# Two norms' last squares summed on TensorE, the samples' exponentials one step later, S5's memsets in two steps

## What is computed

```python
def layer_norm(x, g, b):
    xf = x.astype(jnp.float32)
    mu = jnp.mean(xf, -1, keepdims=True)
    var = jnp.mean(jnp.square(xf - mu), -1, keepdims=True)
    y = (xf - mu) * lax.rsqrt(var + LN_EPS) * g.astype(jnp.float32) + b.astype(jnp.float32)
...
    for layer in range(DEPTH):
        xp = layer_norm(DEEPNORM_ALPHA * xp + 0.5 * swiglu(xp, *f1), ln_g[layer, 0], ln_b[layer, 0])
        ...
            attn = moba_sample(qa, ka, va, cache_k[li], cache_v[li], page_table, pos_s)
        ...
        xp = layer_norm(DEEPNORM_ALPHA * xp + mix_p, ln_g[layer, 1], ln_b[layer, 1])
        xp = layer_norm(DEEPNORM_ALPHA * xp + 0.5 * swiglu(xp, *f2), ln_g[layer, 2], ln_b[layer, 2])
```

## Time and profile before

| | us |
|---|---|
| median of 3 runs | 2454.2 |
| lowest, highest | 2453.1, 2458.01 |
| the profiled execution | 2458.37 |
| its span, first to last instruction | 2456.7 |
| mean granted TensorE clock in it | 0.988 of full speed |

### The profile page before, as it was taken

One profiled execution on the slowest core, in us unless ns is written; L12 is line 12 of the kernel. 1 busy time (PEld: TensorE's weight loads), 2 busy tenths in 40 slices (PEclk: granted clock), 3 DMA queues, 4 the chain that ended last, 5 costly groups with the idle time before them and its releaser, 6 DMA issues.

```text
span 2456.7 us, 46764 instructions
## 1 busy us (share of the span) xinstructions
PE 2376.1 (97%) x19043; PEld 2262.7 (92%) x19043; DVE 1633.0 (66%) x2539; ACT 1079.0 (44%) x1632; POOL 463.7 (19%) x531
## 2 busy tenths in 40 slices
PE   9999999999999999999999999999999999999998
PEld 8988998999789878789999999999999998999998
DVE  6898876666665656777677476477556595487555
ACT  3433445433454343442454434454333537354332
POOL 4997700002100012100203001031002010221001
PEclk9999999999999999999999999999999999999999
DMA  8668666445356798544565555555555566555453
GB/s 218 168 185 223 186 195 190 121 117 157 106 149 198 239 311 249 130 131 123 168 173 169 166 180 173 171 167 147 147 154 155 172 196 205 151 168 150 145 152 99
DMA packets 676327, 417.87 MB, mean 170 GB/s; under 512 B 31378, under 2 KB 639602, under 8 KB 676114
## 3 DMA queue, kind: packets, MB, share of 16 engines
q1 hardware_dynamic: 669810, 394.56, 55.7%
q0 software_dynamic: 6304, 20.32, 2.6%
HBM read 396.04 MB, written 18.78 MB: 169 GB/s over the span
## 4 chain that ended last, share of the span: by engine, by line
PE 79%; DVE 13%; ACT 3%; issue 3%; POOL 1%; SPq 0%; DMA 0%; DVEq 0%; ACTq 0%; POOLq 0%
PE ps L271 22%; PE ps L272 21%; PE ps L273 21%; DVE w_lo L266 4%; PE ps L1033 2%; PE ps L1034 2%; PE ps L1035 2%; ACT w_hi L257 2%; PE ps L2442 1%; DVE h_lo L476 1%; PE ps L1770 1%; PE ps L1194 1%; PE ps L2425 1%; PE ps L2388 1%; DVE x L566 1%
## 5 line engine op out<-in xcount | busy, mean ns | idle before, releaser
L266 DVE TENSOR_TENSOR w_lo<-w_raw,w_hi 128x1024 fp32r<-128x1024 f32 (+1 forms) x648 | 831.4, 1287 | 584.4 <-ACT w_hi L257 581.2
L271 PE MATMUL ps<-x_hi,w_hi 128*128 128x256 f32 (+1 forms) x3200 | 967.7, 302 | 23.0 <-DVE w_lo L266 17.4
L272 PE MATMUL ps<-x_lo,w_hi 128*128 128x256 f32 (+1 forms) x3200 | 953.0, 298 | 0.0
L273 PE MATMUL ps<-x_hi,w_lo 128*128 128x256 f32 (+1 forms) x3200 | 952.6, 298 | 0.0
L257 ACT ACTIVATE w_hi<-w_raw 128x1024 fp32r<-128x1024 f32 (+1 forms) x648 | 669.9, 1035 | 548.3 <-PE ps L273 478.1
L271 PEld LDWEIGHTS ps<-x_hi,w_hi 128*128 128x128 f32 x3200 | 612.8, 191 | 41.5 <-DVE w_lo L266 28.0
L272 PEld LDWEIGHTS ps<-x_lo,w_hi 128*128 128x128 f32 x3200 | 613.4, 192 | 1.1 <-issue 0.2
L273 PEld LDWEIGHTS ps<-x_hi,w_lo 128*128 128x128 f32 x3200 | 613.2, 192 | 0.0
L271 PE MATMUL ps<-h_hi,w_hi 128*128 128x256 f32 (+1 forms) x1408 | 423.5, 301 | 11.5 <-DVE w_lo L266 8.0
L273 PE MATMUL ps<-h_hi,w_lo 128*128 128x256 f32 (+1 forms) x1408 | 415.1, 295 | 0.0
L272 PE MATMUL ps<-h_lo,w_hi 128*128 128x256 f32 (+1 forms) x1408 | 415.0, 295 | 0.0
(11 more groups left out here) (287 smaller groups left out, 2172.1 us busy)
## 6 DMA issues: line engine op xcount, KB each, us to landing
w_raw<-in_ffn_w_gate SPq DMA_DIRECT2D x176, 512.0 KB, 3.8
w_raw<-in_ffn_w_up SPq DMA_DIRECT2D x176, 512.0 KB, 3.8
w_raw<-in_ffn_w_down SPq DMA_DIRECT2D x128, 512.0 KB, 4.2
w_raw<-in_w_in_ab SPq DMA_DIRECT2D x56, 512.0 KB, 3.8
w_raw<-in_ffn_w_down SPq DMA_DIRECT2D x64, 384.0 KB, 3.5
arena<-in_cache_k SPq DMA_DIRECT2D x64, 256.0 KB, 4.3
arena<-in_cache_v POOLq DMA_DIRECT2D x64, 256.0 KB, 5.1
w_raw<-in_w_out_ab SPq DMA_DIRECT2D x16, 512.0 KB, 4.1
```

What stands on the lines that cost most here:

```text
L266: dve.tensor_tensor(T.w_lo[:, u % RINGS, 0:n], T.w_raw[:, u % RINGS, 0:n], T.w_hi[:, u % RING, 0:n].bitcast(F32), ALU.subtract).then_inc(T ...
L271: pe.matmul(out, w_hi, m_hi, start=first, stop=False)
L272: pe.matmul(out, w_hi, m_lo, start=False, stop=False)
L273: return pe.matmul(out, w_lo, m_hi, start=False, stop=last)
```

## The change

It has three parts. In the norms N0B and N3B, GpSimd adds six squares instead of eight. TensorE waits for these and for the eighth square, multiplies the sum with the ones and then the seventh and eighth square, in the same accumulation: two products more for each norm. In the samples' attention the exponentials move from step 8 to step 9, behind ScalarE's copy of keys of that step, and the totals from step 9 to step 11. The two memsets of S5's preparation, both in step 6 before, stand in steps 8 and 10.

```diff
--- before.py
+++ after.py
@@ -503,8 +503,8 @@
 
     STEPS = 9
 
-    def __init__(self, T, g, row, scale, products, slack=0):
-        self.steps, n = self.STEPS + 3 * slack, slack
+    def __init__(self, T, g, row, scale, products, slack=0, summed=KT):
+        self.steps, n, self.summed = self.STEPS + 3 * slack, slack, summed
         self.square_at, self.var_at, self.root_at = 1 + n, 4 + n, 4 + 2 * n
         self.scale_at, self.round_at, self.rest_at, self.bias_at = 5 + 2 * n, 5 + 3 * n, 6 + 3 * n, 7 + 3 * n
         self.T, self.g, self.row, self.products = T, g, row, products
@@ -515,7 +515,7 @@
         self.added, self.sums, self.centred, self.squared = (
             c.take(k) for c, k in ((T.acc_added, KT - 1), (T.sum_done, 1), (T.centred, KT), (T.squared, KT)))
         self.sq_added, self.var, self.rooted, self.normed = (
-            c.take(k) for c, k in ((T.sq_added, KT - 1), (T.var_done, 1), (T.rstd_ready, 2), (T.normed, KT)))
+            c.take(k) for c, k in ((T.sq_added, summed - 1), (T.var_done, 1), (T.rstd_ready, 2), (T.normed, KT)))
         self.affine, self.rounded, self.ready = (
             c.take(k) for c, k in ((T.affine_done, KT), (T.x_rounded, split), (T.x_ready, split)))
 
@@ -545,8 +545,13 @@
                 pe.wait_ge(T.acc_added.h, self.added + KT - 1)
                 pe.matmul(self.ps, T.ones[:, :], self.acc, start=True, stop=True).then_inc(T.sum_done.h, 1)
             if i == self.var_at:
-                pe.wait_ge(T.sq_added.h, self.sq_added + KT - 1)
-                pe.matmul(self.ps, T.ones[:, :], self.acc2, start=True, stop=True).then_inc(T.var_done.h, 1)
+                pe.wait_ge(T.sq_added.h, self.sq_added + self.summed - 1)
+                if self.summed < KT:
+                    pe.wait_ge(T.squared.h, self.squared + KT)
+                mm = pe.matmul(self.ps, T.ones[:, :], self.acc2, start=True, stop=(self.summed == KT))
+                for k in range(self.summed, KT):
+                    mm = pe.matmul(self.ps, T.ones[:, :], T.sq[:, k % 4, 0:self.g.n], start=False, stop=(k == KT - 1))
+                mm.then_inc(T.var_done.h, 1)
             yield
 
     def vector(self, dve):
@@ -604,7 +609,7 @@
         for i in range(self.steps):
             if i in (self.square_at, self.square_at + 1):
                 for k in self.half(i, self.square_at):
-                    if k == 0:
+                    if k == 0 or k >= self.summed:
                         continue
                     pool.wait_ge(T.squared.h, self.squared + k + 1)
                     if k > 1:
@@ -1943,7 +1948,7 @@
             bp = self.at(s, 8)
             if bp is not None:
                 self.soft(dve, bp)
-            bp = self.at(s, 9)
+            bp = self.at(s, 11)
             if bp is not None:
                 self.total_of(dve, bp)
             yield
@@ -1974,7 +1979,7 @@
                 act.activation(self.prob_new[tok, :], self.new_turned, ACT.Copy).then_inc(T.sa_p_moved0.h, 1)
             if s < BP * PAGES:
                 self.move_keys(act, lambda out, src: act.activation(out, src, ACT.Copy), s, 0)
-            bp = self.at(s, 8)
+            bp = self.at(s, 9)
             if bp is not None:
                 self.exps(act, bp)
             bp = self.at(s, 18)
@@ -2187,7 +2192,8 @@
                 for t in range(CL):
                     last = dve.tensor_copy(self.falling[:, :, t], S.powers[:, :, CL - 1 - t])
                 last.then_inc(S.fallen.h, 1)
-                for n in range(2):
+            for n in range(2):
+                if i == self.FALL + 2 + 2 * n:
                     T.dve_chain(dve, dve.memset(self.kernel[n][0:GH, :, 0:P], 0.0))
             q = self.at(i, 3)
             if q is not None:
@@ -2887,7 +2893,7 @@
         f0b = parts(F0B, (0,))
         made = ((S.rows_stored, 16 * KT), (S.decays_stored, 64 * KT), (S.taps_stored, 16 * CL * KT))
         PA = Project(T, M, A, w_in, range(SECTIONS), M.by, N0A.ready, made)
-        N0B = Norm(T, B, 0, 2.0, True)
+        N0B = Norm(T, B, 0, 2.0, True, summed=6)
         f0b += parts(F0B, (1, 2), N0B)
         there = ((T.moved, PA.moved + 8), (T.staged, PA.staged + 2 * SECTIONS))
         att_a = Attend(T, M, A, A.tiles, ROWS_AT, there + ((T.k_stored, M.k_stored[A]),))
@@ -2932,7 +2938,7 @@
         N4A = Norm(T, A, 4, 2.0, True, slack=1)
         OA2 = Out(T, A, s5_w_out, s5_w_gate, N3A.affine + KT, N4A, ((S.rested, KT),))
         F2B = Ffn(B, ffn_2, N2B.ready, N2B.affine + KT)
-        N3B = Norm(T, B, 3, 2.0, False)
+        N3B = Norm(T, B, 3, 2.0, False, summed=6)
         f2b = parts(F2B, (0, 1, 2), N3B)
         F3A = Ffn(A, ffn_3, N4A.ready, N4A.affine + KT)
         f3a = parts(F3A, (0, 1))
```

## The result

| | before | changed |
|---|---|---|
| median of the runs, us | 2454.26 | 2440.33 |
| lowest, highest | 2453.1, 2458.01 | 2437.88, 2443.05 |
| the profiled execution | 2458.37 | 2441.55 |
| its span | 2456.7 | 2439.9 |
| mean granted clock in it | 0.988 | 0.991 |

The ratio is 0.9944 with an interval of 0.9931 to 0.9957: 13.9 us faster, 10.6 to 16.9. The forecast was 2439.5.

The account below looks back on a forecast made before the run. TensorE, busy 97% of the span, was taken as the bound, so only its waits and low clock could be won. Terms 4.15 + 1.0 + 9.5 + 0 = 14.65 us off 2454.2 gave 2439.5 us, range 2434 to 2448.

Parts of the forecast that it names:

- Norm 0 of B: First norm of group B: square root 2.95 us earlier plus 1.2 of clock, 4.15 us gained, bounds 2.5 and 4.7.
- the price of the two added products: In norm N0B: TensorE's two added products with the ones take 0.30 us each, 0.60 together.
- the clock, 1.2 us: Projection behind norm N0B: the low clock moves to the 12 products between two waits, winning 1.2 of 1.7 us.
- Rival 1: Whole kernel: low clock follows the waits, so only waits count, 10.65 us gained, time 2443.5; chance 0.20.
- Norm 3 of B: Norm N3B: square root moves only the 1.03 us ScalarE had waited; 1.0 us gained, bounds 0 and 2.0.
- The exponentials: Samples' attention: 6.7 us of key and output waits plus 2.8 of clock, 9.5 us gained, bounds 5 and 10.
- Rival 3: Samples' attention, 831 to 955 us: transfers become the limit, 6.7 us given back, time 2446.2; chance 0.08.
- rival 4: Samples' attention: exponentials come too late, each us costing TensorE one, four times; up to 2460.8 us; chance 0.10.
- The memsets: S5's preparation: VectorE sets the stretch's end, so moving them gains 0 us; bounds +0.5 and -2.2.
- Rival 2: S5's preparation: the memsets do pay as VectorE is not quite the limit; 2.2 us more, time 2437.3; chance 0.07.
- The sign for it that the prediction named: S5's preparation: VectorE without idle time from 105 to 154 us and the same end; an earlier end contradicts the forecast.

Follow-up runs that it names:

- e4: The kernel before with only the two memsets moved to steps 8 and 10; 2456.84 us, ratio 1.0002 to the kernel before.
- e2: The kernel before with six squares summed by GpSimd in norm N0B alone; 2451.63 us, ratio 0.9987 to the kernel before.
- e8: The changed kernel with four copies of 256 columns ahead of each pair's exponentials on ScalarE; 2445.96 us, ratio 0.9960 to the kernel before.
- e9: The changed kernel with S5's two buffers cleared by ScalarE in place of VectorE's memsets; 2440.11 us, ratio 0.9944 to the kernel before.
- e6: The changed kernel with each of S5's two memsets issued five times on VectorE; 2448.26 us, ratio 0.9979 to the kernel before.
- e3: The kernel before with six squares summed by GpSimd in norm N3B alone; 2453.92 us, ratio 0.9997 to the kernel before.
- e10: The changed kernel with VectorE's reciprocal one step earlier in norms N0B and N3B; 2442.13 us, ratio 0.9952 to the kernel before.
- e1: The kernel before with only the exponentials moved to step 9 and the totals to step 11; 2445.23 us, ratio 0.9966 to the kernel before.
- r1: The changed kernel run once more, nothing altered; 2437.8 us, ratio 0.9934 to the kernel before.
- e7: The changed kernel with the samples' totals back in step 9; 2441.24 us, ratio 0.9945 to the kernel before.
- e11: The changed kernel with the edits of e10 and e9 together; 2439.29 us, ratio 0.9936 to the kernel before.
- e12: The changed kernel with VectorE's reciprocal one step earlier in norm N3B alone; 2442.59 us, ratio 0.9946 to the kernel before.

## Why the prediction was right, and where it was not

**Norm 0 of B, 4.15 predicted.** The order of events came as written: the stall at 0.48 (0.5 forecast), the wait ahead of the projection at 3.45 (3 to 4), the low clock on the 12 products between the waits. Two terms of the sum were mis-sized.

The first is the price of the two added products, put at 0.30 us each from the earlier trace rows. Four instructions of line 553 take 1.24 us from the first start to the last end. The last two of them alone are this row:

```profile
613.16 0.70 PE L553 MATMUL ps<-arena,ones 128*128 128x320 f32 x2
```

So they follow each other at (1.24 - 0.70) / 2 = 0.27 us, and a product of two costs 0.54. The 0.30 had counted one of the two instructions; the rest of the second lies behind the modelled start of the next product, and shows as that product's 0.52 us where its neighbours have 0.28, in the earlier trace rows as in the timeline above. Two products cost 1.08 in place of 0.60, which is 0.48 of the 0.61 by which the square root came short (2.34 forward, not 2.95); the rest is small: the product ahead of them took 0.64 (611.98 to 612.62). The rule given ahead, that a matmul costs the distance to the start of the next, thus holds in a row of like products, and not where a product of rounded values follows one of unrounded values.
The page FP8 and Floating Point Precision of the Trainium skill (TensorE Precision Notes) says four passes for true FP32. The trace agrees: a 256-column product of rounded values takes 0.11 to 0.12 from its start to the next (613.82 to 613.93), so by an estimate four passes over 320 columns would be 4 x 0.11 x 320 / 256 = 0.55, or 0.60 with 0.12, and 0.54 was measured. The prediction had set this rule aside on the strength of a misread row.

The second is the clock, 1.2 us. That the low stretch falls between the waits is not the change's doing: e4, with the old norm, has it there, and e2, with the new one, has it behind. The profile that the prediction was read from was the one of four with the old norm that paid it. So this 1.6 us (the -1.6 of the table) belongs to the execution, and what the norm gave is 2.3 against the profile before and 1.8 against the other three, under the lower bound of 2.5. Rival 1 was right for this norm, by another way: the clock was not there to be won. Its reason, that every stall over 2.5 us is followed by a low clock, misread the trace before: one of 2.68 us at 246.91 is not (last section).

**Norm 3 of B, 1.0.** Right in size and reason: -1.0 in seven traces, bounded by the table load, and the next stall grew, by 1.14, as forecast.

**The exponentials, 9.5.** Right: 8.3 timed alone (6.1 to 10.6), 10.4 to 10.6 by the shift. The waits gave 3.7 + 3.4 - 0.34 = 6.8 for 6.7. The clock gave more than the 2.8 put down. The second of its two windows starts at 915.60, in the middle of a low stretch: from 914 to 918 us the clock is 0.57, so 4.0 x 0.43 = 1.7 was there to be won and not 1.1, and the two make 3.4. With 6.8 that is 10.2 of the 10.4 to 10.6. Rival 3 falls by the 301 GB/s and by the waits, none of which is for a transfer, rival 4 by the 0.34; its price of one us for one us held in e8, its clock on top did not at waits of 1.6 us, and waits of 2 us were not made. That the margin is thin was not said strongly enough: in the changed kernel the exponentials end 0.05 us ahead of TensorE's start in the second and third pair (862.65 to 862.70, 901.73 to 901.79), and where TensorE does wait, in the first, the distance is the same (823.52 to 823.57). Nothing is left there.

**The memsets, 0.** Right within what could be told: 0 by e4's time, and the same sum of waits in shorter pieces; the estimate at e9, with the clock added back, has the moved memsets some 0.9 us ahead on average (-1.3 and -0.3), inside the bounds of +0.5 and -2.2. The forecast of 2.6 for the first stall was 1.6 in the changed kernel, 2.6 in e4 and e6. Rival 2, a gain of 2.2, falls by e6, where VectorE has no room, and is not borne out by e9, where even without the memsets the time shows no gain. The sign for it that the prediction named, no earlier end of the stretch, was too fine for one profile: from 95 to 154 us the shift was -1.9 in the changed kernel, and -1.7 in e3, which has the memsets where they were.

**The sum.** 14.65 was forecast. With the corrected terms it is 1.8 to 2.3 + 1.0 + 9.9 + 0 = 12.7 to 13.2 (9.9: -10.5 less the mean of the four without the part, -0.6), inside the interval of 10.6 to 16.9 for the 13.9 measured. So the time came out within 1 us of the forecast although its total was some 1.5 to 2 us high; that closeness is luck, as the measurement leaves 3 us to either side. The four parts timed alone sum to 8.3 + 3.2 + 0.7 - 0.5 = 11.7, each with some 2 us of its own uncertainty: the parts add up.

## What to carry to other kernels

A long block on a second engine, here 2.1 us of exponentials ahead of a weight rounding, costs what it holds up, and not what it is: move it behind the next thing that others wait for, and count in the trace how much time is left before its own reader asks. Ahead of a sum that the matrix engine waits for, let that engine take the last terms itself, and price the added products by a stretch of several of them in a row, never by the distance to a neighbour. Spreading work of a saturated engine moved its waits about; their sum stayed (8.1 and 8.0 us here). And ahead of reading a gain of 1 to 2 us off one pair of profiles, lay the granted clock of the same stretch beside it.

## What the runs showed of the hardware that was not expected

**The same wait is followed by a low clock in one execution and not in another.** Behind unchanged code, before and e2, timeline and the window behind:

```profile
1138.82 0.39 PE L271 MATMUL ps<-h_hi,w_hi 128*128 128x256 f32 x1 [1.60 <-DVE h_lo L476]
...
1140.00:1145.00 5.00, 5.00 (x24) 4.78 (x23) 4.81 (x10) 0.59 (x1) 1.39 (x2) 0.50 0.59 157
```

```profile
1135.42 0.38 PE L271 MATMUL ps<-h_hi,w_hi 128*128 128x256 f32 x1 [1.59 <-DVE h_lo L476]
...
1137.00:1142.00 5.00, 5.00 (x41) 4.69 (x40) 4.82 (x10) 1.25 (x2) 1.39 (x2) 1.00 0.72 185
```

The idle time, its cause and the work around it are alike; the granted clock is 0.50, the lower level of 1.2 GHz, in the one and full in the other. Of 14 profiles, before and e4 paid it, and between the marks at 1132 and 1160 us the other twelve are each 3.0 us shorter than these two. No run here shows what decides it. The length of the wait alone does not, as a longer one shows, TensorE's for GpSimd ahead of line 2154, before and in e4:

```profile
246.91 0.29 PE L2154 MATMUL ps<-arena 64*16 64x128 f32 x2 [2.68 <-POOL arena L2243]
...
247.00:252.00 5.00, 5.00 (x54) 4.64 (x54) 0.78 (x1) 0.00 (x0) 4.57 (x5) 1.00 0.65 128
```

```profile
246.25 0.29 PE L2154 MATMUL ps<-arena 64*16 64x128 f32 x2 [2.66 <-POOL arena L2244]
...
247.00:252.00 5.00, 5.00 (x38) 4.38 (x35) 0.12 (x1) 0.00 (x0) 4.57 (x6) 0.66 0.75 140
```

All 14 profiles have this wait, of 2.65 to 2.70 us. In six of them (e3, e4, e6, e8, e9, e10) a low clock follows, and the shift grows by 1.3 to 1.6 us between the marks at 245.7 and 254; in the other eight it changes by less than 0.2.

**Such places make the spread of single executions.** The stretch between the marks at 154.17 and 254.00 us, in which S5's tables are prepared, has the same work in every kernel. Its length goes with its mean granted clock:

```
granted clock   kernels                            length, us
1.000           before, e1, r1                     99.8 to 100.4
0.983           after, e2, e4, e6, e7, e10, e11    101.1 to 102.3
0.967           e3, e9, e12                        103.7 to 103.9
0.936           e8                                 106.1
```

So the memsets' part could not be read from one pair of profiles.

**A low clock between two waits for the same engine cost nothing here.** In the changed kernel's projection the slow 12 products shorten the second wait to 1.10; in e2 they ran fast, the wait was 2.14 and the low clock came behind it, where it cost the 1.5 us. A mean clock does not tell the two apart; the place of the low stretch does.

**The same small operation of VectorE takes 0.28 or 1.27 us.** A product of 16 x 128, before and after:

```profile
197.63 0.28 DVE L2199 TENSOR_TENSOR arena<-ident,s_skip 16x128 f32<-16x128 f32 x1
```

```profile
198.66 1.27 DVE L2205 TENSOR_TENSOR arena<-ident,s_skip 16x128 f32<-16x128 f32 x1
```

It takes 0.28 in nine of the 14 profiles and 1.25 to 1.32 in the other five (after, e3, e8, e9, e12). GpSimd was between two products of 128 x 512 and 128 x 576 in the first and amid a pair of 128 x 576 in the second. That this is the cause was not separated.
